# Attention inside a mixer: half-size filling steps, a fused bias and maximum, and a softmax queued in two parts

## The reference, cut to what matters

```python
def hybrid_mixer(x, w_in, b_in, conv_w, ...):
    proj = x @ w_in + b_in
    (qa, ka, va, beta_raw, a_raw, za, qb, kb, vb, qc, kc, vc) = jnp.split(proj, split_at, axis=-1)
    o_a = gated_deltanet(qa, ka, va, beta_raw, a_raw, za, conv_w, ...)   # conv of 4 taps + silu on q, k, v
    o_b = chunk_relpos_attention(qb, kb, vb, rel_bias)
    o_c = swa_sink_attention(qc, kc, vc, sinks)
    gates = jax.nn.sigmoid(x @ w_gate + b_gate).reshape(b, t, N_BRANCH, d)
    merged = (gates[:, :, 0] * (o_a @ w_br_a) + gates[:, :, 1] * (o_b @ w_br_b)
              + gates[:, :, 2] * (o_c @ w_br_c))
    return merged @ w_out

def swa_sink_attention(q, k, v, sinks):      # 8 heads of 64, two groups of keys
    s = q k^T * D_C ** -0.5
    s = s - slopes * abs(dist)               # alibi, slope 2^-(h+1)
    s = jnp.where(valid, s, -inf)
    p = softmax(concatenate([s, sink]))[..., :-1]
    return p @ v
```

## Time and profile before

| | |
|---|---|
| median of 3 runs | 2442.34 us (2440.43 to 2442.58) |
| the profiled execution | 2438.52 us, its span 2436.7 us |
| TensorE (PE) busy | 2355.4 us, 97% of the span |
| VectorE (DVE) busy | 1407.7 us, 58% |
| ScalarE (ACT) busy | 1079.3 us, 44% |
| GpSimd (POOL) busy | 132.3 us, 5% |
| mean granted TensorE clock | 0.985 |

### The profile page before, as it was taken

The page is one execution under the profiler, slowest core; times in us unless marked ns, Lnnn a source line. Parts: engine busy times, 40 slices in busy tenths (PEclk is TensorE's granted clock), DMA queues, the critical chain, the costliest instruction groups (busy, mean ns, idle before and its releaser), DMA issues.

```text
span 2436.7 us, 31328 instructions
## 1 busy us (share of the span) xinstructions
PE 2355.4 (97%) x12981; PEld 1949.9 (80%) x12981; DVE 1407.7 (58%) x1911; ACT 1079.3 (44%) x1507; POOL 132.3 (5%) x206
## 2 busy tenths in 40 slices
PE   7999998999999999999988999999999999898999
PEld 6888797877788878888887777888888888676887
DVE  4455557747655455454666667555476554755553
ACT  4444345435444434443345444444444444435542
POOL 2000000010000000000000110000000000340000
PEclk9999998999999999999998999999999999999999
DMA  7556452435555556556533346555536555402654
GB/s 242 196 175 201 144 184 87 138 123 173 190 175 197 181 176 208 184 191 190 169 105 127 114 137 207 183 197 193 190 133 205 175 197 182 161 1 70 207 169 142
DMA packets 207677, 403.27 MB, mean 165 GB/s; under 512 B 13524, under 2 KB 20944, under 8 KB 207536
## 3 DMA queue, kind: packets, MB, share of 16 engines
q1 hardware_dynamic: 200912, 380.91, 47.2%
q0 software_dynamic: 6624, 20.37, 2.9%
HBM read 399.90 MB, written 1.32 MB: 165 GB/s over the span
## 4 chain that ended last, share of the span: by engine, by line
PE 84%; DVE 9%; ACT 5%; DMA 1%; issue 1%; POOL 0%; SPq 0%; ACTq 0%; DVEq 0%
PE PS L430 24%; PE PS L432 23%; PE PS L431 23%; PE PS L447 2%; DVE WL L1224 2%; PE PS L427 2%; PE PS L429 2%; PE PS L428 2%; PE PS L736 1%; DVE QX L1443 1%; ACT PP L935 1%; ACT WH L893 1%; DMA RW<-in_w_ff_in 1%; DVE ZA L1739 1%; DVE SX L1361 0%
## 5 line engine op out<-in xcount | busy, mean ns | idle before, releaser
L1224 DVE TENSOR_TENSOR WL<-RW,WH 128x1024 fp32r<-128x1024 f32 (+2 forms) x736 | 863.9, 1213 | 247.2 <-ACT WH L893 238.6
L893 ACT ACTIVATE WH<-RW 128x1024 fp32r<-128x1024 f32 (+2 forms) x736 | 747.3, 1043 | 503.5 <-PE PS L432 224.9
L430 PE MATMUL PS<-WH,XTH 128*128 128x512 f32 (+3 forms) x1856 | 730.8, 394 | 7.3 <-DVE WL L1224 4.9
L432 PE MATMUL PS<-WH,XTL 128*128 128x512 f32 (+3 forms) x1856 | 716.6, 386 | 0.0
L431 PE MATMUL PS<-WL,XTH 128*128 128x512 f32 (+3 forms) x1856 | 715.1, 385 | 0.0
L430 PEld LDWEIGHTS PS<-WH,XTH 128*128 128x128 f32 x1856 | 354.5, 191 | 89.7 <-DVE XTL L1235 8.2
L432 PEld LDWEIGHTS PS<-WH,XTL 128*128 128x128 f32 x1856 | 354.1, 191 | 75.5
L431 PEld LDWEIGHTS PS<-WL,XTH 128*128 128x128 f32 x1856 | 355.1, 191 | 68.6
L430 PE MATMUL PS<-WH,HTH 128*128 128x512 f32 x688 | 271.9, 395 | 0.0
L432 PE MATMUL PS<-WH,HTL 128*128 128x512 f32 x688 | 270.8, 394 | 0.0
L431 PE MATMUL PS<-WL,HTH 128*128 128x512 f32 x688 | 269.7, 392 | 0.0
(11 more groups left out here) (424 smaller groups left out, 1920.1 us busy)
## 6 DMA issues: line engine op xcount, KB each, us to landing
RW<-in_w_ff_in SPq DMA_DIRECT2D x256, 512.0 KB, 4.6
RW<-in_w_ff_out SPq DMA_DIRECT2D x128, 512.0 KB, 4.6
RW<-in_w_in SPq DMA_DIRECT2D x56, 512.0 KB, 4.3
RW<-in_w_gate SPq DMA_DIRECT2D x48, 512.0 KB, 4.2
RW<-in_ffn_down SPq DMA_DIRECT2D x44, 512.0 KB, 5.0
RW<-in_ffn_gate SPq DMA_DIRECT2D x40, 512.0 KB, 4.8
RW<-in_ffn_up SPq DMA_DIRECT2D x40, 512.0 KB, 4.8
RW<-in_w_out SPq DMA_DIRECT2D x16, 512.0 KB, 5.4
```

What stands on the lines that cost most here:

```text
L430: self.e.matmul(o, xh, wh, start=start, stop=False)
L432: return self.e.matmul(o, xl, wh, start=False, stop=stop)
L893: self.e.activation(u.hi_out, raw, ACT.Copy).then_inc(*self.s["hi"].up(u.n))
L1224: self.e.tensor_tensor(u.lo_out, raw, u.hi_out.bitcast(F), ALU.subtract).then_inc(*self.s["lo"].up(u.n))
```

## The change

- The walk of the nine items is no longer `pipeline` but a new method `attend`. An item has four stages: `softmax_start` ends the first, and `softmax_end` with `att_scale` is a stage of its own. A round is: scores and start of the new item; `fill(1)`; output of the item two before; `fill(1)`; end and scaling of the new item; turn of the item before; `fill(1)`.
- `cols` can give a unit in two steps, each with half of its matmuls (`steps=2`), and the part with z passes on every yield of `rows`. In this stage `fill` takes an entry of `todo` at every second call only; from `others` on at each call, as before.
- Bias and maximum of kind c become one instruction per head, `tensor_tensor_reduce`, which adds the table to the scores, writes the sum and accumulates the maximum, starting from 8 times the sink (`SK`, made once per mixer by a small instruction, `sinks`). The reduction over all heads and the instruction that folded the sink in go.
- The table comes ready multiplied for each of the eight heads (`ALB`, 1 MB). It is loaded once per mixer by GpSimd in `rel_begin`, behind the three bias loads and ahead of the mask addition. The blocks `ali1` and `ali0` leave the constants.
- The first tap of the convolution moves from VectorE to ScalarE (`conv_first`), queued for the four blocks of a part right behind their `conv_in`.
- The first writes to the gates' tiles wait for the last convolution block.

```diff
-        self.e.tensor_scalar(k.QX[:, j, :], k.QP[:, j, 3:259], cw[3], None,
-                             ALU.mult).then_inc(*self.s["gdn_v"].up((l, "cv", j, 0)))
+        self.wait_ge("proj_a", (l, "tap", j))
         for i in range(3):
-            self.wait_ge("gdn_v", (l, "cv", j, i))
+            if i:
+                self.wait_ge("gdn_v", (l, "cv", j, i))
...
+    def conv_first(self, l, j):
+        k = self.k
+        self.wait_ge("proj_a", (l, "q", j))
+        self.e.activation(k.QX[:, j, :], k.QP[:, j, 3:259], ACT.Copy,
+                          scale=k.vec["conv", l, 3][:, j:j + 1]).then_inc(*self.s["proj_a"].up((l, "tap", j)))
...
     def alibi(self, A, bks):
...
+        self.wait_ge("d_ali", A.l)
+        self.wait_ge("att_v", (A.l, "sk"))
         for n, h in enumerate(A.hs):
-            ins = self.e.scalar_tensor_tensor(out=A.soft[:, n, :], in0=al, scalar=-8.0 * 2.0 ** -(h + 1),
-                                              in1=A.sv[n], op0=ALU.mult, op1=ALU.add)
+            ins = self.e.tensor_tensor_reduce(out=A.soft[:, n, :], in0=k.ALB[:, h, 2 * P - A.nk:2 * P], in1=A.sv[n], scale=1.0,
+                                              scalar=k.SK[:, h:h + 1], op0=ALU.add, op1=ALU.max, accum_out=A.max[:, n:n + 1])
         ins.then_inc(*self.s["att_v"].up((A.id, "ali")))
 
     def softmax_start(self, A):
-        self.wait_each(A.soft_ready)
-        self.e.tensor_reduce(A.max, A.soft, AX, ALU.max).then_inc(*self.s["att_v"].up((A.id, "max")))
         if A.sink is not None:
-            self.wait_ge("att_v", (A.id, "max"))
-            self.wait_ge(self.k.small_slot["sinks", A.l], "landed")
-            self.e.scalar_tensor_tensor(out=A.max, in0=A.max, scalar=A.scale, in1=A.sink, op0=ALU.mult,
-                                        op1=ALU.max).then_inc(*self.s["att_v"].up((A.id, "max2")))
-            self.wait_ge("att_v", (A.id, "max2"))
-            self.e.tensor_scalar(A.neg, A.max, -1.0, None, ALU.mult).then_inc(*self.s["att_v"].up((A.id, "neg")))
-            self.e.tensor_tensor(A.es, A.sink, A.max, ALU.subtract).then_inc(*self.s["att_v"].up((A.id, "es")))
+            self.wait_ge("att_v", (A.id, "ali"))
+            self.e.tensor_scalar(A.neg, A.max, -A.scale, None, ALU.mult).then_inc(*self.s["att_v"].up((A.id, "neg")))
+            self.wait_ge("att_v", (A.id, "neg"))
+            self.e.tensor_tensor(A.es, A.sink, A.neg, ALU.add).then_inc(*self.s["att_v"].up((A.id, "es")))
...
+        self.e.dma_start(k.ALB.rearrange("p h n -> p (h n)"), a["consts"][:, C_ALI:NTABLE]).then_inc(
+            *self.s["d_ali"].up(l, by=16))
...
-    def cols(self, w, c0, nt, bks, x):
+    def cols(self, w, c0, nt, bks, x, steps=1):
         for k0 in range(0, 8, KU):
             u = self.take(wsrc(w, k0, KU, c0, nt * P))
-            self.e.cols_part(u, k0, nt, bks, x)
-            self.free(u)
-            yield
+            for n in range(steps):
+                self.e.cols_part(u, k0, range(n * KU // steps, (n + 1) * KU // steps), nt, bks, x)
+                if n == steps - 1:
+                    self.free(u)
+                yield
...
+    def attend(self, gens, fill):
+        gens, ended, turned = list(gens), None, None
+        while gens or ended or turned:
+            new = gens.pop(0) if gens else None
+            if new:
+                next(new)
+            fill(1)
+            if turned:
+                next(turned)
+            fill(1)
+            if new:
+                next(new)
+            if ended:
+                next(ended)
+            turned, ended = ended, new
+            fill(1)
...
         e.softmax_start(A)
-        e.softmax_end(A)
         if A.kind == "b":
             self.drop(b, ("att_a", (A.id, "exp")))
+        yield
+        e.softmax_end(A)
         e.att_scale(A)
         yield
...
-                    for n, _ in enumerate(self.rows(w_in, 8, 1536, [(0, 264, b0), (264, 256, b1)], self.x)):
-                        if n % 2:
-                            yield
+                    yield from self.rows(w_in, 8, 1536, [(0, 264, b0), (264, 256, b1)], self.x)
...
+                for j in range(4 * part, 4 * part + 4):
+                    e.conv_first(l, j)
...
-                if todo:
+                state["steps"] += 1
+                if todo and state["steps"] % state["every"] == 0:
                     todo.pop(0)()
...
-        self.pipeline(gens, fill, 1)
+        e.sinks(l)
+        self.attend(gens, fill)
```

More of the change, by code:

```diff
@@ L36 @@
 NCONST = C_ONE + P
+C_ALI = NCONST
+NTABLE = C_ALI + 8 * 2 * P
 def shape_constants():
@@ L62, in shape_constants @@
         half[f"t{s}"] = level(s, b, a)
-    out = np.zeros((P, NCONST), np.float32)
+    out = np.zeros((P, NTABLE), np.float32)
+    near = np.where((i < 64) & (j >= 64), -NEG, abs(i - j))
+    before = np.where((i >= 64) & (j < 64), -NEG, abs(P + i - j))
+    for h in range(8):
+        out[:, C_ALI + 2 * P * h:C_ALI + 2 * P * h + 2 * P] = -8.0 * 2.0 ** -(h + 1) * np.concatenate([before, near], 1)
     for n, name in enumerate(CHALF):
@@ L376, in step @@
         return self
-    matmul = transpose = activation = tensor_tensor = tensor_scalar = scalar_tensor_tensor = step
+    matmul = transpose = activation = tensor_tensor = tensor_scalar = scalar_tensor_tensor = tensor_tensor_reduce = step
     tensor_copy = tensor_reduce = bn_stats = bn_aggr = reciprocal = memset = dma_start = then_inc = wait_ge = step
@@ L405 @@
     silu_gate = hidden = rel_begin = value_b = key_query = query_c = kv_out = kv_swap = kv_swapped = nothing
-    decays = z_gate = z_inputs = conv_in = conv_silu = square = sums = roots = nothing
-    scores = scores_c = alibi = softmax_start = softmax_end = att_scale = att_turn = att_turned = att_out = split_out = nothing
+    decays = z_gate = z_inputs = conv_in = conv_first = conv_silu = square = sums = roots = nothing
+    scores = scores_c = sinks = alibi = softmax_start = softmax_end = att_scale = att_turn = att_turned = att_out = split_out = nothing
     gate_bias = gate = branch_out = branch_a_out = gate_a = nothing
@@ L465, in rows_part, with cols_part @@
             ins.then_inc(*self.s["mm"].up(*ended))
-    def cols_part(self, u, k0, nt, bks, x):
+    def cols_part(self, u, k0, kks, nt, bks, x):
         k = self.k
         self.wait_ge("lo", u.n)
-        for kk in range(KU):
+        for kk in kks:
             kt = k0 + kk
@@ L1344, in z_inputs, with sinks @@
                              ALU.add).then_inc(*self.s["proj_v"].up((l, "ba", t)))
+    def sinks(self, l):
+        k = self.k
+        self.wait_ge(k.small_slot["sinks", l], "landed")
+        self.e.tensor_scalar(k.SK, k.small["sinks", l], 8.0, None, ALU.mult).then_inc(*self.s["att_v"].up((l, "sk")))
     def alibi(self, A, bks):
         k = self.k
[L1350 to L1351 removed]
         self.wait_ge("mm", bks[1].full)
[L1353 removed]
+        self.wait_ge("d_ali", A.l)
+        self.wait_ge("att_v", (A.l, "sk"))
@@ L2477, in inputs_a @@
                 bks = [self.bank() for _ in range(4)]
-                yield from self.cols(w_in, 512 * part, 4, bks, self.x)
+                yield from self.cols(w_in, 512 * part, 4, bks, self.x, steps=2)
                 for j in range(4 * part, 4 * part + 4):
@@ L2485, in inputs_a @@
                         todo.append(lambda j=j: e.conv_silu(l, j))
+                for j in range(4 * part, 4 * part + 4):
+                    e.conv_first(l, j)
                 if part == 1:
                     todo.extend(norms())
-        state = {"gen": inputs_a(), "spent": False}
+        state = {"gen": inputs_a(), "spent": False, "steps": 0, "every": 2}
         def fill(n):
@@ L2538, in others @@
                     self.drop(g[t], ("gate_v", (l, "a", half, t, "g")))
-        state["gen"], state["spent"] = others(), False
+        state["gen"], state["spent"], state["every"] = others(), False, 1
         fill(1)
```

14 lines of the change are left out of this document (8 added, 6 removed).

## The result

| | before | after |
|---|---|---|
| median of the runs | 2442.15 us (2440.43 to 2442.58) | 2475.78 us (2473.12 to 2479.43) |
| the profiled execution, its span | 2438.52, 2436.7 us | 2473.12, 2471.3 us |
| TensorE busy | 2355.4 us, 97% | 2369.6 us, 96% |
| VectorE busy | 1407.7 us | 1391.9 us |
| ScalarE busy | 1079.3 us | 1089.9 us |

The changed kernel is slower: ratio 1.0141, 95% interval 1.0127 to 1.0155, some 34 us. VectorE has 16 us less work and ScalarE 11 us more, as the edits say. TensorE executes the same instructions and is busy 14 us longer, at a lower mean clock.

What follows compares the result with a forecast made beforehand. The prediction took TensorE as the bound, idle or slow-clocked in both first mixers. Per mixer 4.2 us from the walk, plus 1.4, minus 1.3 gave 4.3, both 8.7: 2433 us from a median of 2442.3, range 2405 to 2446.

Steps and rivals of the forecast that it cites:

- the walk: Engine queues of one mixer followed in emitted order from the first scores: w_in ends at about 84.5 us, gate_sums at 102.9.
- the waits for L942: Sign: TensorE's waits at the attention output for ScalarE's copy of turned probabilities fall from 18.1 to under 8 us.
- The dense product's new wait for the split of Oc: Sign: first matmul of a part waits for VectorE's split of the item before, some 5 us in each mixer.
- The wait at call 25: At the 25th filling call in the attention, the dense product waits for the last item's bias: 3.8 us.
- VectorE's waits for ScalarE's cut: Sign: in the attention stage these waits come to 10 us or more.
- gate_sums comes no earlier: Failed sign: gate_sums was to come about 3 to 5 us earlier after the first scores.
- The load on GpSimd: The extra 1 MB table load behind three bias loads costs nothing; it would cost only if it took 60 us.
- The prediction's sum of TensorE's work up to the end of w_in: Filling steps, turns, scores and outputs of one mixer at full clock: 67.5 us, against 86.4 measured.
- The fused instruction: Bias and maximum in one: six reductions of 0.72 us go, 5.5 us of VectorE with small instructions, against 1.3 added.
- The tap on ScalarE: First convolution tap moved: VectorE loses 4.6 us for 12 blocks, ScalarE gains 4.3 us, in front of the next cut.
- the gain in the attention: Each mixer was to gain 4.3 us, both 8.7: 4.2 by the walk, plus 1.4, minus 1.3.
- The rival for a slower kernel: ScalarE's exponentials, conv_in and taps ahead of the cut: VectorE waits 26 us, not 16; 2452 us; chance 0.13.

Runs made afterwards that it cites:

- after_8steps: The changed kernel with the ninth convolution block taken before the gate steps, so 8 gate steps and not 9 lie ahead of delta: 2444.18 us, ratio 1.0012.
- after_copy_first_fill3: The changed kernel with delta's copy gPW queued ahead of the fill and three filling steps instead of four between delta's halves, nine steps kept: 2441.37 us, ratio 1.0000.
- before_fused: The kernel before with only the fused bias and maximum, its table and `sinks`: 2436.27 us, ratio 0.9980.

## Why the prediction was wrong

**The step that failed** is the last of the parts: "One more gate step is eaten before gate_sums (9 conv and square calls are left, not 8); 1.41 us of dense work, which is not lost but done earlier; 64 such steps exist and delta uses 46, so no cover is lost." As an amount this holds: delta uses 46 of the 55 steps that are left. But a filling step also brings, every 4 or 8 steps, the end of its part into the queues of ScalarE and VectorE, and these stand in order with delta's own chain. The step was costed by TensorE's time alone, and the walk stopped at gate_sums. It cost 31.6 us by after_8steps (2475.8 to 2444.2) and 34.4 by after_copy_first_fill3 (to 2441.4), so all or nearly all of the slowdown of 34. It would have been open to see: the walk should have counted the steps modulo 4 into delta and asked which fill, ahead of or behind `level_mid`, holds the part's end. The prediction's last sentence, that a longer delta would say that "the cover was moved and not won", named the place but not the reason: cover was not short, it was out of step.

**What was right.** Of the signs that were named: the waits for L942 fell below 8 us (2.6). The dense product's new wait for the split of Oc came at call 17, in the first mixer 1.11 behind the bias and 3.07 behind the split, 4.2 us where "some 5" stood. (The walk itself had 38.3 to 45.2 for this, 6.9 us.) The wait at call 25 came as 1.07, 0.42 and 1.96, 3.5 us where 3.8 stood. VectorE's waits for ScalarE's cut in the first attention, 352 to 460 us, are 27.4 us, where 10 or more stood and the kernel before has 6.3. The clock there is 0.89, under 0.95 as said. One sign failed: gate_sums comes no earlier. VectorE and ScalarE at call 25 of the changed kernel, as walked: exponentials, four conv_in, four taps, the cut, and VectorE 5.24 us (4.9 in the walk):

```profile
424.93 1.54 ACT L975 ACTIVATE QP<-PS,VEC 128x256 f32<-128x256 f32 x4
426.35 1.70 ACT L981 ACTIVATE QX<-QP,VEC 128x256 f32<-128x256 f32 x4
427.95 1.05 ACT L899 ACTIVATE WH<-RW 128x1024 fp32r<-128x1024 f32 x1
...
429.04 1.22 DVE L1236 TENSOR_TENSOR WL<-RW,WH 128x1024 fp32r<-128x1024 f32 x1 [5.24 <-ACT WH L899]
```

The load on GpSimd cost nothing. Its row, the counterpart of the earlier trace rows, shows 11.1 us to landing, and no instruction waited for it:

```profile
ALB<-in_consts POOLq DMA_DIRECT2D x2, 1024.0 KB, 11.1
```

**Terms with the wrong size.** The walk had the last w_in step 84.5 us behind the first scores and gate_sums at 102.9. TensorE's timeline of the changed kernel, with the gaps of call 17 (first scores at 352.44; counterpart of the earlier trace rows):

```profile
391.63 1.10 PE L560 MATMUL PS<-PT,VC 128*64 128x128 f32 x8 [2.66 <-DVE Ob L1404]
...
399.51 0.58 PE L433 MATMUL PS<-XTH,WH 128*128 128x256 f32 x1 [3.07 <-DVE Oc L1404]
...
440.18 0.40 PE L436 MATMUL PS<-WH,XTH 128*128 128x512 f32 x1
...
459.71 0.37 PE L585 MATMUL PS<-SX,CO 128*128 128x8 f32 x2
```

These give 87.7 and 107.3. Two things are missing in the prediction. One is the output's wait of 2.66 us for the split of Ob, which it does not name: ScalarE's half of this split stands behind four exponentials and two cuts, VectorE's behind its own two cuts. (The kernel before has such waits too, but short ones, 1.1 us at the most.) The other is the clock of TensorE: I priced the opening and the end of the stage at full speed and the waits by their length. Behind each of three gaps close together (2.66, 1.11, 3.07) TensorE is at the lower of its two levels (the first matmul of a product takes 0.58 where the earlier trace rows has 0.38, the eight of an output 1.10 where the earlier trace rows has 0.66), and that time is in no wait. The window's mean of 0.89 says the same: the gaps moved, and the clock did not rise.

The walk of VectorE came closer. From 377.8, its 25.4, to the end of the eighth chain at 441.0 VectorE waited 17.8 us where 16.1 stood, and the work with its small gaps took 45.4 where 43.3 stood. So the chain ends at 88.6 in the walk's time, not at 84.8. Which of the two engines set the 3.2 us by which w_in ended late was not separated. (The prediction's sum of TensorE's work up to the end of w_in adds up to 67.6 us, 67.8 without its rounding, and not to 67.5. Nothing hangs on that.)

**The parts.** The fused instruction takes 343 ns at 128 columns and 474 at 256 (0.3 and 0.45 predicted), and its cost above the bias alone is less than the 0.08 a head that I took: starts 0.40 apart where the earlier trace rows has 0.37 for bias alone. Its worth is another matter: I had 4.2 us of VectorE in each mixer, 8.4 for both, and the run changed by 4.9 us in the old order and by 10.7 in the new. The tap on ScalarE I had as 4.6 us off VectorE against 4.3 on ScalarE, and counted for it by the walk; the runs say that with 8 steps it costs 4.6 us in sum, and that with 12 no price can be told. The first fits what the walk itself found, VectorE waiting behind ScalarE's conv_in, taps and cut, but I never walked the order without the taps, so the term's sign stayed hidden. The new loop with its half steps was the core of the change. Against before_fused (2436.3), after_8steps is 7.9 us slower; 4.6 of it are the taps, so about 3.3 us are left to the loop and to the ninth block taken early, which were not separated. With the fused instruction at its 10.7 us of the new order, the loop would be charged more.

So of the 34 us, 31.6 are the phase of the parts' ends, and the rest is, by one way of sharing it out at 8 steps, the sum of -4.9 (fused), +4.6 (taps) and about +3 (order). The sharing doesn't carry over to another phase: with 12 steps ahead of delta the changed kernel is faster than the kernel before (0.9982, 0.9973 to 0.9992), and its median is 4.6 us below that of the kernel before with 12 steps too, though there the intervals overlap a little. The second step that failed is therefore the size of the gain in the attention. With the phase set right the changed kernel stands between 2436.6 and 2444.2 us, where 2433 was forecast: the walk's 102.9 us to gate_sums came as 107.3. The rival for a slower kernel had its own mechanism (ScalarE's queue in the attention, 10 us of waits more in each mixer); this is not what happened, since VectorE's waits were 17.8 us and not 26, and gate_sums comes no later than before (107.3 against 107.1 us, with one gate step more in it). That the kernel came out slower speaks for neither of the two.

## What to carry to other kernels

Filling work is not only time on the bound engine: at the end of each of its parts it puts instructions of other engines into queues that a latency chain uses too. Whoever adds, drops or moves one filling step ahead of such a chain should follow the count through it and look where the parts' ends fall; the first, cheap experiment is the same kernel with one to three steps more. And a gain in one stage should be measured with the phase of the next one held fixed, else the two are read as one.

## What the hardware showed

- A fused add and maximum with an accumulator (`tensor_tensor_reduce`) appears as two instructions, and the second is all but free. VectorE in the changed kernel (counterpart of the earlier trace rows):

```profile
393.85 0.47 DVE L1373 CUSTOM_DVE_ANT_0 SC<-ALB,PS,SX 128x256 f32<-128x256 f32 x1
394.25 0.08 DVE L1373 DVE_READ_ACCUMULATOR2_ANT SX<- 128x1 f32 x1
394.25 0.47 DVE L1373 CUSTOM_DVE_ANT_0 SC<-ALB,PS,SX 128x256 f32<-128x256 f32 x1
```

  The next head starts at the same 394.25 as the accumulator's read, so a head costs 0.40 us, against 0.37 for the bias alone and some 0.36 more for the maximum that goes. The Trainium skill's "VectorE: DVE Perf Modes", section "Two Vector instructions with no wait between them", counts such an operation as two instructions, and the rows agree; that the read costs no time of its own here, they add.
- ScalarE's copy of 128x256 takes 516 ns from SBUF (L981, 24 of them, 507 to 533) and 470 from PSUM (L975, 24, 454 to 497; counterpart of the earlier trace rows). The Trainium skill's "VectorE: DVE Perf Modes", section "The TRN2 errata — SBUF-src ops pay a fixed extra latency per instruction", gives ScalarE a fixed term of 224 cycles from SBUF and 172 from PSUM, at 1.2 GHz; by that I estimate 43 ns, and the rows' 46 agree. With one cycle a column on top, that table of the Trainium skill comes to 400 and 357 ns by my estimate. The durations are longer, but the distance of two starts agrees: by the rows at call 25 four taps follow one another in 1.60 us and four conv_in in 1.42, so 0.40 and 0.355 us each. The prediction took 0.36 for both.
- A small gap can cost more than its length: behind the 2.43 us at 494.50 the 32 small matmuls of L650 take 1.98 us, and 1.15 where no gap stood ahead. It doesn't each time. The output behind the wait for Ob took 1.10 us in the changed kernel, and in after_8steps, behind a wait of the same length, 0.66:

```profile
391.71 0.66 PE L560 MATMUL PS<-PT,VC 128*64 128x128 f32 x8 [2.65 <-DVE Ob L1404]
```

  Delta's windows lost 10 us of work each by waits and clock together (0.96 and 0.93 for 1.00).
